# A two-part fp32 network on one core: the last attention's queries split tile by tile inside their projection, and another order of small steps at the layer ends

## The chip, the cores and the metric

The kernel runs on one core of a Trainium2 chip. A core has a matmul engine (TensorE, PE in the rows), a vector engine (VectorE, DVE), a scalar engine for activations (ScalarE, ACT), GpSimd (POOL), and SyncE (SP), which here issues the transfers. Each engine works through its own instructions in order; they meet at semaphores. The metric is the device time of one execution in microseconds. The matmul engine's clock is granted by a throttle and shown by the profile as a share of full speed: 1.00 is 2.4 GHz, 0.50 is 1.2 GHz.

## What is computed

Two blocks of a network in float32, with 512 tokens of width 1024 (and in the second block 256 context tokens). Shortened from the reference:

```python
def first_block(x, ...):
    h = x
    h = h + recurrent_block(h, ...)   # rmsnorm, w_in, gelu, causal conv, RG-LRU, w_out
    h = h + swiglu(h, ...)            # f0
    shared = shared_kv(h, ...)        # keys and values, plain and compressed
    h = h + nsa_layer(h, ..., *shared)  # w_in, q norm, rope, three attentions, w_out
    return h + swiglu(h, ...)         # f1

def rg_lru(x, gate_w, gate_b, lam):
    ...
    log_a = -LRU_C * jax.nn.softplus(-lam.astype(jnp.float32)) * r
    a = jnp.exp(log_a)
    ...

def modulate(x, shift, scale):
    return rms_norm(x) * (1 + scale) + shift

def odd_mixer(a_lat, a_ctx, rows, cols, w_in, sinks, w_out, ctx_out):
    ...
    q, k, v = split(a_lat @ w_in, s)  # 16 query heads, 2 key/value heads of 64
    q = axial_rope(q, rows, cols)
    k = axial_rope(k, rows, cols)
    ...
    o_lat, o_ctx = swa_heads(q, k, v, qc, kc, vc, sinks, ctx_out)
    return o_lat @ w_out, ...
```

The second block has an even layer (multi-head latent attention, MLA, and neighbourhood attention, NA, side by side, one output projection, swiglu g0), and an odd layer (sliding-window attention, SWA, over blocks of 128 queries, output projection, swiglu g1), then a last norm. Shifts, scales and gates of its layers come from `c` and `c_ctx` through the 6144-wide `mod_w`, the modulation.

## The kernel before

**Number form.** Every matmul takes its operands split into a high part, rounded to fp32r, and a low part, the rest. `mm3` makes three matmuls of one product (high by high, high by low, low by high), all recorded at L507.

**Weights.** They come as slabs of 128x1024 floats, 512 KB each. SyncE loads them in a fixed order into four places `RAW`; ScalarE's `high` (L430) writes the rounded half to `WH`, VectorE's `low` (L436) the rest to `WL`. `plan_of_weights` lists the slabs in their order. A call of `high` or `low` splits all slabs up to the one that `Slabs.upto` gives, three slabs ahead of the one it names. SyncE waits before each load until the last user of the place is done. Of the slabs, 96 are `mod_w`: they aren't split but read three times by VectorE in `mod_step` (L457, L460, L463), which does the modulation's product; `mod_passed` on ScalarE only goes past one in the order of splits. These steps stand inside the loops of f0, kv, the compression, b_out and f1.

**Order.** Each engine's program is written out by hand, stage by stage: functions `*_tensor`, `*_scalar`, `*_vector` are called in turn at the end. The stages are lru (`a_in`, gates, conv, scan, `a_out`), f0, kv, compression, q (`b_in`), nsa, b_out, f1, even (`e_in`, `e_v`, `q_up`), mla, na, e_out, g0, odd (`o_in`), swa, o_out, g1, out. `linear` makes one output tile of 128 features by up to 512 tokens, in one of three PSUM places; another engine must evacuate it before the place is used again.

**Lru.** VectorE evacuates `a_in` tiles 8 to 15 into the convolution (L972 to L978), then waits for ScalarE's Abs and Exp of lambda (L916, L918), runs a chain of small operations that makes `-8 softplus(-lam)` (L990 to L1015), and then evacuates the tiles of the gelu branch (L1029).

**Layer ends.** The last output projection of a stage runs by token parts. `turn_scalar` and `turn_vector` handle its end: `residual` (L700, L702) adds the PSUM tile to `H`; `square` (L638) and a matmul with ones give the sum of squares, `root` (L659, L662) the inverse root, and the loop over `kt` of 0 to 7 makes the normalised tiles (`normed_scaled` L682, `normed_high`, `normed_low`) that the next stage's first matmuls take. Between these steps the loop holds, for the next token part, the residuals of tiles 6 and 7 (at kt 2 and 5), the squares of tiles 5, 6, 7 (at kt 1, 3, 6), and the splits of the next slabs (at kt 1 and 4). In f1's last chunk `even_ahead_vector` and `even_ahead_scalar` prepare the context tokens of the even layer; the context itself is loaded once the last modulation step has left its vector's place.

**MLA and NA.** Both run rounds of scores, softmax, transposes and output. The first slabs of `e_out` are split by the call for `("mla_w", 0)` at s = 46 near the end of NA, between its softmax steps. `NB`, the neighbourhood biases, are loaded before the first of `e_out`'s late loads.

**Odd and SWA.** `o_in` gives tile 8 (keys), tiles 0 to 7 (two query heads each) and 9 (values). ScalarE copies a tile to a ring of three `TMP` places, VectorE makes its rotary form (L1093, L1095, L1097) in `QRAW2`. At the start of SWA `split_queries` makes 16 high halves on ScalarE (`query_high`, L1331) and 16 low halves on VectorE (`query_low`, L1336) into `Q2`. SWA then has 64 rounds, one for each block of queries and head: scores (L507), maximum (L2425), exponentials (L1393), transposes (L1402), evacuation (L1409), output, and flips of the outputs (L1436, L1442).

## Time and profile before

| | us |
|---|---|
| median of 3 runs | 3247.99 |
| the runs | 3247.99, 3265.96, 3245.41 |
| the profiled execution | 3253.99 |
| its span (first to last instruction) | 3251.9 |
| granted TensorE clock, mean over it | 0.965 |

The busy shares of the page say how much of the span each engine works; the shares of an engine that nothing waits for cost nothing. The chain is the work that ended last, followed back. In a timeline row the first number is the start in us from the span's start, the second the duration, and in brackets stands the engine's idle time just before, with what ended it. A trace is one execution; its terms are compared with its own time of 3253.99.

### The profile page before, as it was taken

Reading aid. Unit: us, or ns where it says so; the run is one execution under the profiler, and the core shown is the slowest. Engines: PE = TensorE matmul, PEld = TensorE weight load, DVE = VectorE, ACT = ScalarE, POOL = GpSimd, SP = SyncE. Lnnn points to the kernel's source line nnn. Section 1 sums busy time; section 2 is a strip of 40 time slices with the busy share of each in tenths; the row PEclk is TensorE's granted clock in tenths of the full one; section 3 lists DMA queues with packets and bytes.
Section 4 is the critical chain, followed back from the end, with each engine's and each line's share of the span. In section 5 each row is a group of like instructions: output and inputs, shape, how many; then the busy total and the mean of one; then the engine's idle time right before and its main releaser. Section 6 shows DMA issues by size and latency. Waiting matters only on the chain.

```text
span 3251.9 us, 41133 instructions
## 1 busy us (share of the span) xinstructions
PE 3032.2 (93%) x16349; PEld 2583.4 (79%) x16349; DVE 1656.7 (51%) x2849; ACT 1178.6 (36%) x2057; POOL 281.4 (9%) x274
## 2 busy tenths in 40 slices
PE   7899999888888999999898989999999989999999
PEld 5688888766778878878678878888888879888887
DVE  6756666656776666641345745222222645443333
ACT  3532223434663322241345643112112445432222
POOL 2310001001562000010000101000000100010001
PEclk9999999988999999999999989999999979999999
DMA  3235444240002445431000011111111200022231
GB/s 139 85 110 168 153 156 142 88 144 33 1 1 91 151 150 173 147 119 49 1 1 18 29 52 66 65 65 58 66 65 60 65 27 1 20 85 97 92 102 66
DMA packets 76287, 260.19 MB, mean 80 GB/s; under 512 B 8257, under 2 KB 12865, under 8 KB 75969
## 3 DMA queue, kind: packets, MB, share of 16 engines
q1 hardware_dynamic: 76096, 257.57, 23.9%
q8 instruction: 130, 2.13, 0.3%
q14 instruction: 61, 0.49, 0.0%
HBM read 255.44 MB, written 2.10 MB: 79 GB/s over the span
## 4 chain that ended last, share of the span: by engine, by line
PE 76%; DVE 8%; issue 6%; ACT 6%; POOL 2%; DMA 2%; DVEq 0%; SPq 0%; POOLq 0%; ACTq 0%
PE PS L507 73%; PE PS L1402 2%; POOL PB L1754 1%; ACT WH L430 1%; DVE WL L436 1%; DVE SM L2425 1%; DMA RAW<-in_f_in 1%; DVE TMP L682 1%; PE PS L1436 0%; ACT TMP L1409 0%; PE PS L1581 0%; ACT TMP L1393 0%; DVE RAW L463 0%; DMA RAW<-in_a_in 0%; ACT PB L1409 0%
## 5 line engine op out<-in xcount | busy, mean ns | idle before, releaser
L430 ACT ACTIVATE WH<-RAW 128x1024 fp32r<-128x1024 f32 (+1 forms) x367 | 379.4, 1036 | 859.5 <-PE PS L507 543.8
L507 PE MATMUL PS<-UH,WH 128*128 128x512 f32 (+1 forms) x1664 | 603.4, 363 | 52.3 <-DVE UL L962 12.4
L436 DVE TENSOR_TENSOR WL<-RAW,WH 128x1024 fp32r<-128x1024 f32 (+1 forms) x367 | 448.3, 1224 | 361.9 <-ACT WH L430 350.3
L507 PE MATMUL PS<-UL,WH 128*128 128x512 f32 (+1 forms) x1664 | 591.6, 356 | 0.0
L507 PE MATMUL PS<-UH,WL 128*128 128x512 f32 (+1 forms) x1664 | 588.6, 354 | 0.0
L507 PEld LDWEIGHTS PS<-UH,WH 128*128 128x128 f32 x1664 | 318.1, 191 | 108.8 <-DVE WL L436 31.1
L507 PEld LDWEIGHTS PS<-UL,WH 128*128 128x128 f32 x1664 | 318.1, 191 | 47.6 <-issue 5.8
L507 PEld LDWEIGHTS PS<-UH,WL 128*128 128x128 f32 x1664 | 317.0, 191 | 45.2
L648 POOL TENSOR_TENSOR ACC<-ACC,TMP 128x256 f32<-128x256 f32 (+1 forms) x108 | 115.0, 1080 | 2140.8 <-ACT TMP L638 2139.3
L507 PE MATMUL PS<-XSH,WH 128*128 128x512 f32 (+1 forms) x752 | 285.7, 380 | 15.3 <-DVE WL L436 5.8
L507 PE MATMUL PS<-XSL,WH 128*128 128x512 f32 (+1 forms) x752 | 284.2, 378 | 0.0
L507 PE MATMUL PS<-XSH,WL 128*128 128x512 f32 (+1 forms) x752 | 284.1, 378 | 0.0
L507 PE MATMUL PS<-HH,WH 128*128 128x512 f32 (+1 forms) x698 | 239.5, 343 | 2.6 <-DVE HL L2294 2.6
L507 PE MATMUL PS<-HL,WH 128*128 128x512 f32 (+1 forms) x698 | 239.1, 343 | 0.0
L507 PE MATMUL PS<-HH,WL 128*128 128x512 f32 (+1 forms) x698 | 237.5, 340 | 0.0
L835 DVE TENSOR_TENSOR TMP<-TMP,PS 128x512 f32<-128x512 f32 (+1 forms) x88 | 66.3, 753 | 301.1 <-PE PS L507 227.9
L702 DVE SCALAR_TENSOR_TENSOR H<-PS,MOD,H 128x512 f32<-128x512 f32 (+1 forms) x105 | 63.0, 621 | 242.5 <-PE PS L507 242.5
L507 PEld LDWEIGHTS PS<-XSH,WH 128*128 128x128 f32 x752 | 143.3, 191 | 43.5 <-DVE WL L436 10.6
L507 PEld LDWEIGHTS PS<-XSH,WL 128*128 128x128 f32 x752 | 143.2, 190 | 25.9
L507 PEld LDWEIGHTS PS<-XSL,WH 128*128 128x128 f32 x752 | 143.3, 191 | 25.5
L507 PEld LDWEIGHTS PS<-HH,WH 128*128 128x128 f32 x698 | 132.5, 190 | 19.4 <-DVE HL L2294 3.0
L507 PEld LDWEIGHTS PS<-HH,WL 128*128 128x128 f32 x698 | 132.1, 189 | 15.8
(349 smaller groups left out, 5396.9 us busy)
## 6 DMA issues: line engine op xcount, KB each, us to landing
RAW<-in_mod_w SPq DMA_DIRECT2D x96, 512.0 KB, 3.3
RAW<-in_f_in SPq DMA_DIRECT2D x88, 512.0 KB, 3.3
RAW<-in_g_in SPq DMA_DIRECT2D x88, 512.0 KB, 3.2
RAW<-in_f_out SPq DMA_DIRECT2D x32, 448.0 KB, 4.0
RAW<-in_g_out SPq DMA_DIRECT2D x32, 448.0 KB, 3.1
RAW<-in_a_in SPq DMA_DIRECT2D x16, 512.0 KB, 3.6
RAW<-in_f_out SPq DMA_DIRECT2D x16, 512.0 KB, 4.3
RAW<-in_g_out SPq DMA_DIRECT2D x16, 512.0 KB, 3.2
```

What stands on the lines that cost most here:

```text
L430: act.e.activation(hi, raw, ACT.Copy).then_inc(wh.step(n, i), 1)
L436: dve.e.tensor_tensor(lo, raw, hi.bitcast(F32), ALU.subtract).then_inc(wl.step(n, i), 1)
L507: return pe.e.matmul(out, l, r, start=start, stop=stop)
L648: pool.e.tensor_tensor(ACC[:, a:z], ACC[:, a:z], TMP[:, (kt - 1) % 3, a:z], ALU.add).then_inc(acc.step(key, p, kt), 1)
L682: dve.e.scalar_tensor_tensor(TMP[:, kt % 4, a:z], Hh[:, kt, a:z], gain(kt, a), RS[:, a:z], ALU.mult, ALU.mult).then_inc(xs.step(key, kt, p ...
L702: dve.e.scalar_tensor_tensor(Hh[:, m, a:z], o[:, c], g(m, a), Hh[:, m, a:z], ALU.mult, ALU.add).then_inc(res.step(stage, m, a), 1)
L835: dve.e.tensor_tensor(TMP[:, 2, 0:N], TMP[:, j % 2, 0:N], psum.at[tile][:, 0:N], ALU.mult).then_inc(dve_f.step(name, "mul", j), 1)
L1402: t = pe.e.transpose(o[:, 128 * j:128 * j + 128], b[:, col - lo:col - lo + 128], con("ident"))
L1754: pool.e.tensor_tensor(p, p, r.unsqueeze(2).to_broadcast([128, c, L]), ALU.mult).then_inc(scaled.step("nsa", n), 1)
L2425: dve.e.tensor_reduce(stat_of(n)[:, 0:1], psum.at["score", "swa", n][:, a:z], AX.X, ALU.max, negate=True).then_inc(most.step("swa", n), 1)
```

## The change

1. Lru: on both engines, one more slab, `a_in` 11, is split before the root. Abs and Exp of lambda go to the start of ScalarE's program, and VectorE's chain of small operations from behind the convolutions to before them.
2. Turns: the next part's residuals of tiles 6 and 7 at kt 0 and 2, its squares at kt 0, 2, 4, behind the splits of the next slabs, which go to kt 0 and 1.
3. Modulation: f1 holds 25 steps in its first loop where it held 32, none after j = 19; seven steps go to the q stage, one beside each of `b_in` 1 to 7.
4. Transfers: the last constants are loaded in front of `f1_in` 3 and no longer behind the context. Three `e_out` slabs are loaded in front of the biases.
5. Late in f1 VectorE prepares the context before the residuals, and ScalarE squares its last tile behind `normed_high`.
6. The look-ahead splits of `e_out` 0, 1, 2 go from s = 46 of NA to s = 9, 20, 31 of MLA.
7. Odd and SWA: the rotary form stays in the `TMP` ring, and each tile's two queries are split inside the `o_in` loop into `Q3`, a place of its own. `SKR` and `OST2` get other places; the flips and `OX` use `Q3`. Copies and evacuations wait accordingly.

Shortened to its core (VectorE's side is like ScalarE's, with `low` for `high`; the moved chain of lambda is not shown again):

```diff
+def mods_of(name, j):
+    if name == "f1":
+        return 0 if j > 19 else 2 if j % 3 == 0 and j > 3 else 1
+    return 2 if j % 3 == 0 or j in (10, 16) else 1
...
-    split("b_in", *range(9))
+    for i in range(9):
+        split("b_in", i)
+        if 0 < i < 8:
+            mod()
...
-    SKR = at("SKR", V0 + 15 * KB, [128, 768])
-    QRAW2 = at("QRAW2", V0 + 24 * KB, [128, 8, 512])
-    OST2 = at("OST2", V0 + 40 * KB, [128, 1024])
+    SKR = at("SKR", T0 + 12 * KB, [128, 768])
+    Q3 = at("Q3", V0 + 16 * KB, [128, 4, 16, 128], F32R)
+    OST2 = at("OST2", U0 + 44 * KB, [128, 1024])
...
+            if j == after("f1_in", 22):
+                sp.wait_ge(fin.after("nsa", 3, 3, 1))
+                sp.e.dma_start(CON[:, NC2:CONST_N], consts[:, NC2:CONST_N]).then_inc(s_con3, 16)
             if j == after("mod_w", 95):
                 sp.wait_ge(mod.after(95, 2))
                 sp.e.dma_start(CB, ctxT).then_inc(s_ctx, 16)
-                sp.wait_ge(fin.after("nsa", 3, 3, 1))
-                sp.e.dma_start(CON[:, NC2:CONST_N], consts[:, NC2:CONST_N]).then_inc(s_con3, 16)
...
     def turn_scalar(act, key, stage, Xd, shift, free, slabs_next):
...
-                if p + 1 < n and kt in (1, 3, 6):
-                    square(act, key, {1: 5, 3: 6, 6: 7}[kt], p + 1, h_ready, [])
                 if (p - n, kt) in slabs_next:
                     high(act, *slabs_next[p - n, kt])
+                if p + 1 < n and kt in (0, 2, 4):
+                    square(act, key, 5 + kt // 2, p + 1, h_ready, [])
...
     def turn_vector(dve, key, stage, tiles, g, h_before, Xd, gain, shift, free, slabs_next):
...
-                if p + 1 < n and kt in (2, 5):
-                    residual(dve, stage, tiles[1 + (kt == 5)], 6 + (kt == 5), p + 1, g, h_before)
                 if (p - n, kt) in slabs_next:
                     low(dve, *slabs_next[p - n, kt])
+                if p + 1 < n and kt in (0, 2):
+                    residual(dve, stage, tiles[1 + kt // 2], 6 + kt // 2, p + 1, g, h_before)
...
-        return {(-2, 1): (out[0], out[1] + 6), (-2, 4): (out[0], out[1] + 7), **({(-1, 1): first} if first else {})}
+        return {(-2, 0): (out[0], out[1] + 6), (-2, 1): (out[0], out[1] + 7), **({(-1, 1): first} if first else {})}
...
     def lru_scalar(act):
...
         logexp(act)
+        s1 = SM[:, 8:16]
+        act.e.activation(s1, vec("lam", 0, 8), ACT.Abs).then_inc(act_a.step("abs"), 1)
+        act.wait_ge(act_a.after("abs"))
+        act.e.activation(s1, s1, ACT.Exp, scale=-1.0).then_inc(act_a.step("lam"), 1)
...
+        high(act, "gate_w", 0, 1)
         root(act, "a", 0)
...
     def q_vector(dve):
...
+            if 0 < s < 8:
+                mod_step(dve, [dve_q.after("q", s - 3, "rope")] if s > 2 else [])
...
     def mla_scalar(act):
...
+            if s in AHEAD_AT:
+                high(act, "mla_w", 0, AHEAD_AT[s])
+    AHEAD_AT = {9: 2, 20: 1, 31: 0}
...
     def na_scalar(act):
...
-            if s == 46:
-                high(act, "mla_w", 0)
...
     def odd_scalar(act):
...
             if s > 2:
-                act.wait_ge(dve_q.after("o", s - 3, "rope"))
+                act.wait_ge(dve_q.after("o", 0, "rope"), *([dve_q.after("swa", s - 4, 1, "lo")] if s > 3 else []))
...
+            if s > 2:
+                odd_queries_scalar(act, s - 3)
         high(act, "o_in", 9)
+        odd_queries_scalar(act, 6)
+        odd_queries_scalar(act, 7)
...
     def odd_vector(dve):
...
-                roped(dve, "o", i, TMP[:, i % 3, :], 512, con("coss"), con("sins"), QRAW2[:, i - 1, :] if i else SKR[:, 0:512], [])
+                roped(dve, "o", i, TMP[:, i % 3, :], 512, con("coss"), con("sins"), TMP[:, i % 3, 0:512] if i else SKR[:, 0:512], [])
...
+            if 2 < s < 9:
+                odd_queries_vector(dve, s - 3)
         low(dve, "o_in", 9)
+        odd_queries_vector(dve, 6)
+        odd_queries_vector(dve, 7)
...
+    def odd_queries_scalar(act, i):
+        for j, (x, q3) in enumerate(odd_query(i)):
+            query_high(act, "swa", i, j, x, q3, [dve_q.after("o", i + 1, "rope")])
...
     def swa_scalar(act):
...
-        split_queries("swa", QRAW2, lambda i: [dve_q.after("o", i + 1, "rope"), lin.after("o_in", 9)], "act", act)
```

## Rows read from the trace of the kernel before

**Rows 1.** The page: busy us by engine, then engines' shares of the chain that ended last.

```profile
PE 3032.2 (93%) x16349; PEld 2583.4 (79%) x16349; DVE 1656.7 (51%) x2849; ACT 1178.6 (36%) x2057; POOL 281.4 (9%) x274
...
PE 76%; DVE 8%; issue 6%; ACT 6%; POOL 2%; DMA 2%; DVEq 0%; SPq 0%; POOLq 0%; ACTq 0%
```

**Rows 2.** Timeline of TensorE, recurrent layer: start, us, engine, line, operation, idle before and releaser.

```profile
40.55 0.77 PE L507 MATMUL PS<-UH,WH 128*128 128x512 f32 x1 [8.03 <-DVE TMP L972]
...
100.50 0.77 PE L507 MATMUL PS<-UH,WH 128*128 128x512 f32 x1 [9.49 <-DVE Y L1029]
```

**Rows 3.** Timeline of TensorE: the first and the last of four turns.

```profile
193.28 0.36 PE L507 MATMUL PS<-UH,WH 128*128 128x256 f32 x1 [3.21 <-DVE H L700]
...
2876.97 0.55 PE L507 MATMUL PS<-XSH,WH 128*128 128x256 f32 x1 [3.70 <-DVE H L702]
```

**Rows 4.** Timeline of TensorE, f1: first and last of three waits, then the turn.

```profile
1077.20 0.50 PE L507 MATMUL PS<-XSH,WH 128*128 128x512 f32 x1 [1.48 <-DVE WL L436]
...
1317.85 0.50 PE L507 MATMUL PS<-XSH,WH 128*128 128x512 f32 x1 [1.33 <-DVE WL L436]
...
1401.57 0.80 PE L507 MATMUL PS<-ACC,CON 128*128 128x256 f32 x1 [5.07 <-POOL ACC L648]
```

**Rows 5.** Timelines of TensorE and ScalarE at the end of NA.

```profile
1900.94 1.12 PE L1436 MATMUL PS<-CON,NBC 128*128 128x128 f32 x4 [8.87 <-ACT RS L1409]
...
1894.70 1.06 ACT L430 ACTIVATE WH<-RAW 128x1024 fp32r<-128x1024 f32 x1 [4.83 <-DMA RAW<-in_e_out]
...
1899.62 0.90 ACT L1393 ACTIVATE TMP<-PS,SM 128x768 f32<-128x768 f32 x1 [2.63 <-DVE SM L2247]
```

**Rows 6.** Timelines of TensorE, ScalarE and VectorE: SWA's start, and one projection tile.

```profile
2652.06 0.58 PE L507 MATMUL PS<-SKH,Q 128*128 128x256 f32 x1 [9.06 <-ACT PB L1393]
...
2638.48 10.42 ACT L1331 ACTIVATE Q<-QRAW 64x512 fp32r<-64x512 f32 x16
...
2639.14 11.45 DVE L1336 TENSOR_TENSOR Q<-QRAW,Q 64x512 fp32r<-64x512 f32 x16 [14.35 <-ACT Q L1331]
...
2600.41 0.69 DVE L1093 TENSOR_TENSOR TMP<-PS,CON 128x512 f32<-128x512 f32 x1 [3.10 <-PE PS L507]
```

**Rows 7.** Windows: stretch, us, busy of PE, PEld, DVE, ACT, POOL, clock, DMA, GB/s.

```profile
193.68:197.09 3.41, 3.41 (x18) 3.41 (x17) 0.61 (x2) 0.30 (x1) 0.00 (x0) 0.50 0.33 127
1900.94:1921.29 20.35, 14.63 (x65) 12.72 (x65) 3.17 (x12) 7.55 (x13) 0.00 (x0) 0.50 0.17 61
2652.06:2671.76 19.70, 19.70 (x95) 19.70 (x96) 6.34 (x17) 8.55 (x25) 0.00 (x0) 0.50 0.00 1
2667.51:2671.05 3.54, 3.54 (x19) 3.54 (x18) 1.05 (x3) 1.44 (x4) 0.00 (x0) 0.50 0.00 0
2686.66:2688.82 2.16, 2.10 (x19) 1.96 (x18) 0.94 (x4) 1.33 (x4) 0.00 (x0) 1.00 0.00 0
```

**Rows 8.** Timelines of VectorE and ScalarE, recurrent layer.

```profile
38.57 1.23 DVE L436 TENSOR_TENSOR WL<-RAW,WH 128x1024 fp32r<-128x1024 f32 x1 [3.29 <-issue]
...
91.85 1.28 ACT L918 ACT_TABLE_LOAD   x1
...
93.38 0.17 DVE L990 TENSOR_SCALAR SM<-SM 128x8 f32<-128x8 f32 x1 [5.50 <-ACT SM L918]
```

**Rows 9.** Timeline of VectorE: the residual ahead of the first turn's wait.

```profile
192.71 0.42 DVE L700 TENSOR_TENSOR H<-PS,H 128x256 f32<-128x256 f32 x1
```

**Rows 10.** The chain that ended last, around the even turn.

```profile
1383.19 6.60 DMA H<-in_ctxT
```

**Rows 11.** Timeline of SyncE's queue as f1 starts.

```profile
1050.03 13.02 SPq L471 DMA_DIRECT2D RAW<-in_f_in  x2
```

**Rows 12.** Timeline of VectorE in the q stage.

```profile
743.34 0.75 DVE L1086 SCALAR_TENSOR_TENSOR TMP<-PS,SM,TMP 128x512 f32<-128x512 f32 x1 [3.33 <-ACT TMP L1081]
```

**Rows 13.** Groups of VectorE by line, 1000 to 1400 us: count, busy, mean ns, idle before.

```profile
L463 DVE CUSTOM_DVE_ANT_1 RAW<-RAW,H,VECS 128x1024 f32<-128x1024 f32 x43 | 55.3, 1285 | 1.5
...
L460 DVE CUSTOM_DVE_ANT_1 TMP<-RAW,H,MOD 128x512 f32<-128x512 f32 x43 | 33.4, 776 | 1.5
```

More of the change, by code:

```diff
@@ L176, in ffn @@
                 if step:
-                    mod()
-                    if j % 3 == 0 or j in (10, 16):
+                    for _ in range(mods_of(name, j)):
                         mod()
@@ L412, in body, with splits_until @@
     split_at = {"act": 0, "dve": 0}
-    def splits_until(which, name, idx):
-        a, z = split_at[which], slabs.upto[slabs.index[name, idx]]
+    def splits_until(which, name, idx, short=0):
+        a, z = split_at[which], slabs.upto[slabs.index[name, idx]] - short
         split_at[which] = max(a, z)
@@ L424, in split_places, with high @@
         return name, idx, hi[:, 0:n], lo[:, 0:n], raw_of(name, idx)[:, 0:n], [] if old is None else [lin.after(*slabs.plan[old][0:2])]
-    def high(act, name, idx):
-        for j in splits_until("act", name, idx):
+    def high(act, name, idx, short=0):
+        for j in splits_until("act", name, idx, short):
             n, i, hi, _, raw, used = split_places(j)
@@ L430, in high, with low @@
             act.e.activation(hi, raw, ACT.Copy).then_inc(wh.step(n, i), 1)
-    def low(dve, name, idx):
-        for j in splits_until("dve", name, idx):
+    def low(dve, name, idx, short=0):
+        for j in splits_until("dve", name, idx, short):
             n, i, hi, lo, raw, used = split_places(j)
@@ L453, in mod_step @@
         low(dve, "mod_w", j)
-        dve.wait_ge(loaded("mod_w", j), act_a.after("cond"), dve_a.after("mod_b", 3))
+        dve.wait_ge(loaded("mod_w", j), act_a.after("cond"), dve_a.after("mod_b", 3), *free)
         if j:
@@ L479, in sync_engine @@
         after = lambda *slab: slabs.issued[slabs.index[slab]]
-        first_late = next(j for j, old in enumerate(slabs.old) if old is not None and slabs.plan[old][0] == "e_out")
+        first_late = next(j for j, old in enumerate(slabs.old) if old is not None and slabs.plan[old][0] == "e_out" and slabs.plan[old][1] > 2)
         for j in range(3, len(slabs.plan)):
@@ L848, in ffn_vector @@
                 low(dve, *tile)
+                if c == 2 and name == "f1":
+                    even_ahead_vector(dve, m)
                 if m < 5 or not ends:
@@ L914, in lru_scalar @@
         gates_scalar(act, 7)
-        s1 = SM[:, 8:16]
-        act.e.activation(s1, vec("lam", 0, 8), ACT.Abs).then_inc(act_a.step("abs"), 1)
-        act.wait_ge(act_a.after("abs"))
-        act.e.activation(s1, s1, ACT.Exp, scale=-1.0).then_inc(act_a.step("lam"), 1)
         act.e.activation(IDR[:, :], con("ident"), ACT.Copy).then_inc(act_a.step("idr"), 1)
@@ L1015, in lru_vector @@
         dve.e.tensor_scalar(NSP, s4, -8.0, None, ALU.mult).then_inc(done, 1)
+        low(dve, "gate_w", 0, 1)
+        low(dve, "gate_w", 1)
+        for m in range(8):
+            b, o = TMP[:, m % 4, :], XR[:, m, :]
+            dve.wait_ge(rstd.after("a", 0))
+            if m > 3:
+                dve.wait_ge(dve_a.after("conv", m - 4, 3))
+            dve.e.memset(b[:, 0:3], 0.0).then_inc(dve_a.step("pad", m), 1)
+            dve.wait_ge(lin.after("a_in", 8 + m))
+            dve.e.tensor_tensor(b[:, 3:515], psum.at["a_in", 8 + m][:, 0:512], RS[:, 0:512], ALU.mult).then_inc(dve_a.step("x", m), 1)
+            psum.leave(("a_in", 8 + m), dve_a)
+            dve.wait_ge(dve_a.after("pad", m), dve_a.after("x", m))
+            dve.e.tensor_scalar(o, b[:, 0:512], vec("conv_w", m), vec("conv_b", m), ALU.mult, ALU.add).then_inc(dve_a.step("conv", m, 0), 1)
+            for k in (1, 2, 3):
+                dve.wait_ge(dve_a.after("conv", m, k - 1))
+                dve.e.scalar_tensor_tensor(o, b[:, k:k + 512], vec("conv_w", 8 * k + m), o, ALU.mult, ALU.add).then_inc(dve_a.step("conv", m, k), 1)
+            low(dve, "a_in", 8 + m)
         def decay(m):
@@ L1452, in flipped_hi @@
     def flipped_hi(q):
[L1453 removed]
+        return lambda m: Q3[:, q, m:m + 4, :]
     def flipped_lo(q):
[L1456 to L1467 removed]
+        return lambda m: Q3[:, q, 8 + m:12 + m, :]
     Wave = namedtuple("Wave", "g q rows L tiles first last")
@@ L2132, in mla_vector @@
                     rotary_low(dve, h + 1)
+            if s in AHEAD_AT:
+                low(dve, "mla_w", 0, AHEAD_AT[s])
     def na_gpsimd(pool):
@@ L2480, in scalar_engine @@
         out_scalar(act, "o_out", "g1", False, of_mods(1, 3), ("g1_in", 0))
-        ffn_scalar(act, "g1", 512, [], "out", False)
+        ffn_scalar(act, "g1", 512, [lin.after("o_out", 7)], "out", False)
         turn_scalar(act, "out", ("g1", 2), None, None, [], next_slabs(("g1_out", 16), None))
```

60 lines of the change are left out of this document (17 added, 43 removed).

## The prediction

> **What bounds the kernel.** I read the page's busy shares and its chain first. The reader is to see that TensorE (PE) is busy 93% of the span of 3251.9 us and carries 76% of the chain; no other engine comes near [rows 1]. So only two things can move the end: time in which TensorE waits, and time in which it runs at the lower of its two clock levels, 1.2 instead of 2.4 GHz. Next I listed, on TensorE's timeline, every wait over 0.35 us with its releaser, and looked in the window view at the granted clock behind each. The large waits are few and each lies in a place that the change touches: two in the recurrent layer's start [rows 2], one at the head of each of four layer turns [rows 3], four in the second feed-forward layer f1 and the turn behind it [rows 4], one at the end of the neighbourhood attention (NA) [rows 5], one at the start of the last attention (SWA) [rows 6]. Behind each, the clock stands at 0.50 for some us: the windows of 3.41 us behind a turn and of 20.35 and 19.70 us behind the two attention waits show it [rows 7].
>
> **The change part by part**, in us gained.
>
> 1. *Split of a_in slab 11 before the root.* TensorE waits 8.03 until 40.55. It starts 0.75 after VectorE's split that ended at 39.80, and that split stood idle for 3.29, since its slab could be loaded only when a_in 11, its place's last user, was split behind the root [rows 2, 8]. With a_in 11 split earlier the load is no longer last; ScalarE's two remaining splits (1.06 each, [rows 5]) and VectorE's 1.23 follow the root, which ends at about 31.3 (8.5 before the VectorE split's end). That gives 31.3 + 2.1 + 1.2 + 0.75 = 35.4, and with 0.7 for the start of the chain 36.1. Gain **4.4** (3.3 to 5.2).
>
> 2. *Lambda's chain to the front.* VectorE idles 5.50 for ScalarE's Abs and Exp, then runs 26 small operations from 93.38 to 98.6, and TensorE waits 9.49 for the evacuation queued behind them [rows 2, 8]. Moved, they lie under the first loads, where both engines have nothing to do. The wait of 9.49 and the 2.2 lost behind it at the half clock go, but the decay and scan work behind it stays as long as it was and TensorE comes to it sooner: its next wait grows by about 3.7 in my reading. Gain **8.0** (4 to 11.7). The moved Abs and Exp need no further table load at the front if they stand in the set that the logarithm has loaded; a load is 1.28 and the Exp starts at its end [rows 8]. By the Trainium skill, "ScalarE: Activation LUTs", "What ACT_TABLE_LOAD costs", a switch is 1.28 us plus a drain of 1.38; the row shows the 1.28 and no drain after it, and by the page the 5.50 would hold 2.66 for the switch instead of 1.28. In both readings it is part of the 5.50 that goes, so it changes the reading of that wait and not the sum.
>
> 3. *Turns: the next part's residuals at steps 0 and 2 instead of 2 and 5, squares likewise.* Four turns wait 3.21, 3.60, 3.22 and 3.70 for the residual of the last tile, 13.7 together [rows 3]. In the first, that residual (0.42 long) starts at 192.71, and the matmul at 193.28 [rows 9]; three steps of the normalising loop earlier is 3 us earlier. I leave 0.7 of each wait: 13.7 - 2.8 = 10.9. Each is followed by 3.41 us at 0.50 [rows 7], which at the full clock take half: 4 x 1.65 = 6.6. The smaller turn behind the odd layer's attention gives 1.5 by its own two waits of 1.6. Sum **19.0**. Below: 0, if the order only passes the wait on (a rival). The splits of the next slabs move from steps 1 and 4 to 0 and 1: 1.2 each on VectorE, ahead of the residual, covered by matmuls that already have their slabs; without that cover it is one split, 1.2, per turn.
>
> 4. *f1 with 25 modulation steps in its loop instead of 32.* Three waits on the low half of a slab's split, from 1.48 to 1.33 with 2.96 between, 5.8 together [rows 4], come where two modulation steps stand between two splits on VectorE. With one step in nearly all iterations they go; the half clock behind the longest gives 1.5. Gain **7.3** (3 to 7.3).
>
> 5. *The even turn.* TensorE waits 5.07 for the sum of squares of the context [rows 4], whose load, 6.60 long, is on the page's chain there [rows 10]. The load waits for the last modulation step, which comes two iterations sooner. The constants' load that stood behind it in the queue goes to 1050 us; there the queue's two issues of 13.02 us are waiting for places, and the transfer engines have nothing [rows 11], so it costs nothing; without that cover it is the 6.60 of the load of the same size. Gain 5.07 and 1.9 of clock, **7.0** (3 to 7).
>
> 6. *e_out's first three splits out of the end of NA.* The wait of 8.87 ends with the last head's exponentials, and ahead of these ScalarE waits 4.83 for e_out's load and then splits, VectorE likewise [rows 5]. Taken away, softmax work is next in line at once. The whole 8.87 goes; of 14.63 us of TensorE work at 0.50 behind it [rows 7], which would take 7.3 at the full clock, I take a little over half of the 7.3, 4.0, since the low clock lasted after each turn too [rows 7]. Gain **12.9** (8.9 to 16.2). The same splits in MLA are three times 1.06 on ScalarE and 1.23 on VectorE, each about half busy there: **-1.5** (0 to -3).
>
> 7. *SWA's query splits into the projection.* Before, 16 splits on ScalarE (10.42) and 16 on VectorE (11.45) stand between the projection and the scores, and TensorE does its first transposes at 2652.06, after a wait of 9.06 for the first exponentials [rows 6]. In the projection VectorE idles 3.10 in each tile [rows 6], so two splits of 0.72 hide; ScalarE, with two of 0.65, has still less to do. Behind the projection two tiles' splits are left beside ScalarE's evacuation and its table load. In before, the first split on ScalarE started behind both of these, at 2638.48 [rows 6]; there the first exponentials can start now, and with 2.0 for them and for what leads to the transposes (estimated from 0.90 for one set of them in the NA rows [rows 5]) these come at 2640.5. Gain 11.5. Behind it TensorE runs 19.70 us at 0.50, in which a round is 3.54 long instead of 2.16 [rows 7]: 5.6 rounds, 7.7 at most. I take **3.0** of it, for the same reason as at NA. Together **14.5** (11.5 to 19.2). The copy of tile s now waits for the split of tile s - 4; behind it on ScalarE stands the evacuation that frees a place for TensorE, but that split is over a tile old by then.
>
> 8. *Seven modulation steps into the q stage* (b_in 1 to 7). A step's three passes are 1.29, 0.78 and, of the same form, 0.78 again, with their starts 2.87 [rows 13]; VectorE idles 3.33 per tile there [rows 12]. It fits with 0.4 to spare: 0 (-5 to +1). *Tail*: the last residuals take their new order there too, where nothing covers them; one residual of 0.42 [rows 9] is the bound, I take **-0.3**.
>
> Sum: 4.4 + 8.0 + 19.0 + 7.3 + 7.0 + 12.9 + 14.5 - 1.5 - 0.3 = 71.3. The profiled run took 3253.99 and would take 3182.7; it is 6.0 above the median of 3247.99, which gives **3176.7 us**.
>
> **Rivals.**
>
> *A: the clock does not follow.* At NA's end and SWA's start the waits go but TensorE goes on at 1.2 GHz: 4.0 + 3.0 back, 3183.7. For it: in [rows 7] TensorE worked 19.70 us without a gap at 0.50 before it rose. Against: it did rise. By the Trainium skill, "TensorE: Matmul & The Clock Gate", "A second HAM failure mode: psum-queue depth-cycling", short idles between groups of matmuls make the clock go back and forth; by that rule the sum would be this rival's 3183.7. No row of before shows such a return in the attention's rounds.
>
> *B: the turns pay elsewhere.* The earlier residuals keep VectorE from a normalised tile that is next in TensorE's order, so each turn's wait returns further on: 19.0 back, 3195.7. For it: VectorE runs both in order. Against: the residual costs 0.42 and the matmuls already handed over last longer.
>
> *C: the q stage overflows.* A modulation step does not fit into 3.33 with its two extra waits, or the slab loads it needs come late: seven times 1 to 2 us, 3190.
>
> *D: SWA's splits still end last*, because the last two queries' splits and the table load follow the projection: 14.5 back, 3191.
>
> *E: slower.* Tile by tile splits thin TensorE's work at SWA's start so that its clock stays at 0.50 through the stage. A round is then 3.54 instead of 2.16 [rows 7]; 64 rounds cost up to 88 us, 3176.7 + 88 = 3265. It outweighs the gain once more than 71.3 / 1.38 = 52 of the 64 rounds run low. Against: the clock rose at 2671.76 after a worse start.
>
> **How the numbers follow.** Forecast 0.55, A 0.20, B 0.12, C 0.05, D 0.05, E 0.03. The low end is the forecast with the upper bounds of parts 2, 6 and 7 (3.7, 3.3 and 4.7), 3165, and 5 more for clock that I gave no term: 3160. The high end takes in A to D and two of them together: 3205. A measurement of this kernel tells about 1%, 32 us, from no change. Faster by more than that needs 32 of the 71.3: all but E and three bad terms at once, 0.90; within 1%, 0.07; slower, 0.03.
>
> **What would show it.** In the profile after: no TensorE wait over 1 us for a residual (L700, L702) at the turns; first wait of 8.03 down to 3 to 4; none of 9.49; the VectorE splits of f1 never last; first flip of NA directly behind its last scores; SWA's first transposes 2 to 3 us behind the projection's end; the granted clock up from 0.965 towards 0.98. Wrong would be: waits of 2 us or more in b_in tiles on mod junk or slabs, a wait on the context's load still over 3, or the clock at 0.50 for 10 us or more at either attention.

## The result: 1.5% faster, and where the time went

The changed kernel's median is 3202.02 us (3195.20 to 3213.82, 4 runs) against 3250.11 for the kernel before. The ratio is 0.9847, with a 95% interval of 0.9802 to 0.9893. Executed again beside other kernels it was 3198.69 us (3188.85 to 3204.78), ratio 0.9845 (0.9821 to 0.9869). The forecast was 3176.7, with a range of 3160 to 3205. So the direction was right and the time lies in the range, 3 to 6 us below its upper end, but 46 to 50 us came where 71 were forecast. The profiled execution took 3198.71 us, with a span of 3196.6.

The page of the changed kernel, the lines that answer to [rows 1]:

```profile
PE 3018.4 (94%) x16349; PEld 2571.3 (80%) x16349; DVE 1659.3 (52%) x2849; ACT 1178.3 (37%) x2056; POOL 286.5 (9%) x274
...
PE 49%; DVE 3%; ACT 3%; issue 2%; DVEq 0%; ACTq 0%
```

The chain here could be followed back over 57% of the span only, so its 49% don't compare with the 76% of before.

TensorE issues the same 16349 matmuls in both kernels, in the same order. That gives the best view of all for such a change: take from both timelines the start of matmul number n, and compare stretch by stretch. The table is worked out from the starts in the two timelines, in us. The sum over all stretches is the difference of the spans, 55.3; those left out come to -0.4.

| matmuls | what lies there | before | after | gain | forecast |
|---|---|---|---|---|---|
| start to 200 | first loads, first projection of lru | 77.4 | 77.0 | 0.3 | 4.4 |
| 200 to 380 | gates' end, gelu tiles | 54.3 | 42.5 | 11.8 | 11.7 |
| 380 to 640 | decay, scan, a_out | 51.7 | 58.5 | -6.8 | -3.7 |
| 640 to 760, 2380 to 2500, 4500 to 4620, 12500 to 12700, 14580 to 14800 | five turns | 127.0 | 113.0 | 14.0 | 19.0 |
| 2900 to 3340 | q stage into nsa | 131.9 | 127.5 | 4.4 | 0 |
| 4620 to 6080 | f1 | 332.4 | 324.5 | 7.9 | 7.3 |
| 6080 to 6240 | even turn | 42.0 | 35.2 | 6.8 | 7.0 |
| 7000 to 8100 | MLA | 178.5 | 187.6 | -9.1 | -1.5 |
| 8100 to 9060 | NA | 167.6 | 149.5 | 18.2 | 12.9 |
| 9060 to 12500 | e_out, g0 | 601.8 | 603.3 | -1.5 | 0 |
| 13060 to 13300 | SWA's start | 51.4 | 33.9 | 17.5 | 14.5 |
| 13300 to 14340 | the rest of SWA | 137.1 | 144.7 | -7.7 | 0 |

Two lines stand out: MLA and the rest of SWA give back 17 us, of which the forecast had 1.5.

TensorE's timeline after shows what became of the waits of [rows 2], [rows 3] and [rows 6]: start, us, engine, line, operation, then idle before and its releaser. The line numbers are the changed kernel's.

```profile
37.27 0.47 PE L517 MATMUL PS<-UH,WH 128*128 128x512 f32 x1 [3.50 <-DVE TMP L1019]
...
49.38 1.22 PE L517 MATMUL PS<-XR,RAW 128*128 128x512 f32 x1 [3.33 <-DVE TMP L1019]
...
135.70 0.79 PE L517 MATMUL PS<-YH,WH 128*128 128x512 f32 x1 [6.90 <-DVE YL L1051]
...
185.85 0.36 PE L517 MATMUL PS<-UH,WH 128*128 128x256 f32 x1 [1.15 <-DVE H L710]
...
2592.79 0.35 PE L517 MATMUL PS<-SKH,Q 128*128 128x256 f32 x1 [0.99 <-ACT VS L2350]
...
2595.80 0.58 PE L517 MATMUL PS<-SKH,Q 128*128 128x256 f32 x1 [1.66 <-ACT PB L1407]
```

The wait of 8.03 is 3.50, that of 9.49 is gone, and 6.90 stands at the next one (2.77 in before). A turn's 3.21 is 1.15. At SWA's start 4.28 and 9.06 have become 0.99 and 1.66. In NA the flips now follow the last scores directly, with waits of 0.78 where 8.87 stood [rows 5].

The new wait in MLA, with what stands before it on ScalarE and VectorE:

```profile
1640.32 0.80 PE L517 MATMUL PS<-CKH,QLH 128*128 128x512 f32 x1 [3.80 <-ACT TMP L1407]
...
1634.26 0.83 ACT L1898 ACTIVATE QRS<-QR 32x768 fp32r<-32x768 f32 x1
1635.12 0.84 ACT L1899 ACTIVATE QRS<-QR 32x768 fp32r<-32x768 f32 x1
1635.98 1.06 ACT L439 ACTIVATE WH<-RAW 128x1024 fp32r<-128x1024 f32 x1
1639.27 0.90 ACT L1407 ACTIVATE TMP<-PS,SM 128x768 f32<-128x768 f32 x1 [2.23 <-DVE SM L2120]
...
1637.14 1.23 DVE L445 TENSOR_TENSOR WL<-RAW,WH 128x1024 fp32r<-128x1024 f32 x1 [3.81 <-ACT WH L439]
1638.28 0.95 DVE L2120 TENSOR_REDUCE SM<-PS 128x1 f32<-128x768 f32 x1
```

Read it backwards. TensorE waits for exponentials, these for a maximum (L2120) on VectorE, and this one stands in order behind the split of an e_out slab, which waits for ScalarE's half. ScalarE makes that half only after two rotary halves of 0.83 us. VectorE has been idle for 3.81 us, and the last matmul of the maximum's scores ended at about 1635.5. A split costs 1.23 us of VectorE; in this round it costs TensorE 3 us.

### The profile page after: what moved, and what is told of

It is laid out like the page before. It is cut to its first block, busy times and chain, and to the rows that moved or that the text cites. A ratio compares the mean times of both kernels' runs of the same rounds, so it can differ in the third digit from the quotient of the medians.

```text
span 3196.6 us, 41132 instructions
## 1 busy us (share of the span) xinstructions
PE 3018.4 (94%) x16349; PEld 2571.3 (80%) x16349; DVE 1659.3 (52%) x2849; ACT 1178.3 (37%) x2056; POOL 286.5 (9%) x274
## 3 DMA queue, kind: packets, MB, share of 16 engines
q8 instruction: 130, 2.13, 0.3%
## 4 chain that ended last, share of the span: by engine, by line
PE 49%; DVE 3%; ACT 3%; issue 2%; DVEq 0%; ACTq 0%
PE PS L517 47%; PE PS L1416 2%; DVE SM L2450 0%; PE PS L1450 0%; ACT TMP L1423 0%; DVE PS L2250 0%; DVE SM L2120 0%; ACT TMP L1407 0%; ACT WH L439 0%; DVE QRS L1905 0%; DVE NKL L2174 0%; ACT PB L1423 0%; ACT PB L1407 0%; ACT N L2159 0%; DVE WL L445 0%
## 5 line engine op out<-in xcount | busy, mean ns | idle before, releaser
L445 DVE TENSOR_TENSOR WL<-RAW,WH 128x1024 fp32r<-128x1024 f32 (+1 forms) x367 | 446.4, 1220 | 340.2 <-ACT WH L439 329.3
L517 PEld LDWEIGHTS PS<-UH,WL 128*128 128x128 f32 x1664 | 316.4, 190 | 45.2
L517 PEld LDWEIGHTS PS<-HH,WH 128*128 128x128 f32 x698 | 132.6, 190 | 19.2 <-DVE HL L2299 2.8
```

Source lines behind the costliest of these rows:

```text
L445: dve.e.tensor_tensor(lo, raw, hi.bitcast(F32), ALU.subtract).then_inc(wl.step(n, i), 1)
L517: return pe.e.matmul(out, l, r, start=start, stop=stop)
```

## The experiments

### The same kernel again, and a trade undone

**The changed kernel once more.**

> The changed kernel once more, unaltered. In its first profile the stage by stage sum gives 55.5 us over before, but holds two long stretches at the lower TensorE clock behind small waits: 10.3 us in MLA (1680.8 to 1691.1) and 20.5 us in SWA (2728.7 to 2749.2), where before's profile has none and 3.4. Theory 1 (these stretches come and go from execution to execution): they are absent or elsewhere here, and the span lies within 3188 to 3212 without a code cause. Theory 2 (they belong to the new order, since the change puts splits in MLA and another place for the queries in SWA): both stand at the same instructions again, 10 and 20 us long.

Measured: 3198.69 us, span of the profile 3186.7. SWA in the window view, its three stretches (matmuls 13060, 13300, 14000, 14340), first in the changed kernel's first profile, then in this one. Columns: stretch, us, busy of PE, PEld, DVE, ACT, POOL, granted clock, DMA share, GB/s.

```profile
2586.95:2620.87 33.92, 30.69 (x242) 29.06 (x242) 11.23 (x32) 17.87 (x50) 0.00 (x0) 0.95 0.01 1
2620.87:2712.85 91.98, 87.58 (x702) 86.12 (x701) 46.75 (x136) 52.12 (x140) 0.00 (x0) 0.94 0.00 1
2712.85:2765.59 52.74, 48.75 (x342) 47.78 (x342) 20.55 (x63) 26.62 (x74) 0.00 (x0) 0.81 0.00 1
```

```profile
2581.34:2621.01 39.67, 36.89 (x242) 36.31 (x242) 11.65 (x32) 18.41 (x50) 0.00 (x0) 0.74 0.00 1
2621.01:2712.31 91.30, 86.29 (x702) 84.89 (x701) 46.64 (x135) 51.51 (x140) 0.00 (x0) 0.96 0.00 1
2712.31:2758.18 45.87, 41.71 (x343) 39.89 (x342) 20.15 (x63) 25.95 (x76) 0.00 (x0) 0.96 0.00 1
```

The waits at SWA's start are equal in both (0.99 and 1.66), yet in one profile the clock is low behind them for 3.4 us and in the other for 20.5. In the last quarter it is the other way round. One and the same code has both, so theory 1 holds for SWA. In MLA it fails: the wait of 3.80 and a low stretch of 10.2 us some 40 us later stand at the same matmuls in both, and 7000 to 8100 takes 187.6 and 188.3. That loss belongs to the code.

**The look-ahead splits back in NA.**

```diff
-            if s in AHEAD_AT:
-                high(act, "mla_w", 0, AHEAD_AT[s])
...
+            if s == 46:
+                high(act, "mla_w", 0)
```

With them the biases are again loaded before the first late `e_out` slab (part 4).

> The changed kernel with the look-ahead splits of e_out 0, 1, 2 back at s = 46 of NA, biases loaded first as in before. Theory 1 (the part is a trade, and its cost in MLA was mis-sized): NA's end loses the 15 us that it gained (its wait of about 8.9 is back), MLA wins back 4 to 5 us, 3.1 of it at the wait of 3.80 before the scores of round 22 and 1.3 at the wait of 2.06; the whole is 10 us slower than the changed kernel. Theory 2 (MLA's loss of 9 us in the first profile is clock alone): the wait of 3.80 stays, MLA's length stays within 2 us of the changed kernel's, and the whole is 15 us slower.

Measured: 3196.66 us (3192.52 to 3197.65), ratio 0.9839 (0.9823 to 0.9856). By stretches NA's end (8880 to 9060) loses 16.8 us and MLA wins 10.4, of which 3.3 is the wait (3.80 against 0.51), 1.2 a second wait at the stage's end (2.06 against 0.89) and the rest low clock at 1640 and 1681. The trade is worth 6.4 us, not 11.4 as forecast. The earlier part of NA (8100 to 8880) takes 3 us more here as well, but over the 13 profiles it varies between 114.4 and 119.9 without regard to where these splits stand, so it is left out. By the whole time nothing of the trade is seen. In the profiled execution this is because SWA took 169.2 us where the changed kernel needed 178.6 and 176.8; for the other executions it is not known. Part 6 of the change, placed as it is, gains nothing that can be told by the whole time. Neither theory had MLA's size right: 10 us hang on it, not 4 to 5.

**The splits in rounds with room.**

```diff
-    AHEAD_AT = {9: 2, 20: 1, 31: 0}
+    AHEAD_AT = {9: 2, 17: 1, 29: 0}
```

> The changed kernel with the three look-ahead splits at s = 9, 17 and 29 of MLA instead of 9, 20 and 31: rounds in which neither ScalarE nor VectorE has a rotary or latent split. Theory 1 (at s = 20 VectorE's split waits in order for ScalarE's, which stands behind two rotary halves of 0.83 us each, and the next round's maximum stands behind both): the wait of 3.80 at about 1640 falls to 0.7 to 1.0, the clock stretch behind it goes, gain 3 to 5 us over the changed kernel. Theory 2 (any round is hurt by a split, each engine being busy half the time): a wait of 2 to 4 us appears in round 18 or 19 instead, no gain.

Measured: 3193.61 us (3183.92 to 3199.53), ratio 0.9830 (0.9806 to 0.9853). MLA takes 180.7 us instead of 187.6. TensorE's wait for the same scores, and the window in which the changed kernel had 0.88 of the clock (second fence):

```profile
1636.09 0.50 PE L517 MATMUL PS<-CKH,QLH 128*128 128x512 f32 x1 [0.51 <-ACT TMP L1407]
...
1640.00:1690.00 50.00, 44.56 (x317) 38.97 (x317) 23.50 (x56) 24.30 (x51) 0.00 (x0) 1.00 0.04 11
```

```profile
1640.00:1690.00 50.00, 45.19 (x281) 39.38 (x281) 22.12 (x53) 23.53 (x50) 0.00 (x0) 0.88 0.09 31
```

3.80 has become 0.51, and with the wait both low stretches went, the one right behind it and the one 40 us later. That is theory 1, and 6.9 us in this stage instead of the 3 to 5 expected. 8.9 were won, 3.3 of them the wait's own and the rest mostly clock, and 2.0 were lost, 1.0 in each of the two rounds that took the splits, where new waits of 1.33 and 1.34 stand (around matmuls 7400 and 7650). No wait of 2 us has appeared there. All seven profiles with a split at s = 20 have 187.1 to 188.7 for this stage, and `flips_apart`, the other one with 9, 17, 29, has 180.8. By the whole time the 5 to 8 us between the medians are not clear of the spread.

### SWA

**The queries split behind the projection again.** The edit takes back `Q3`, the in-loop splits and their waits (part 7 alone).

> The changed kernel with the queries of the last attention kept after rotation and split in one go behind the projection, as in before (places and waits of before too). Theory 1 (the 17.8 us gained at SWA's start in the first profile pair are this part's, and what follows it in SWA is clock by chance): the wait of 9 us and the low clock at the start are back, 15 to 18 us slower than the changed kernel at SWA's start, and the low stretch of 20.5 us in SWA's third quarter is not tied to it. Theory 2 (the query place Q3 is what brings the 6.9 us lost in SWA's second half): the start loses 17 and the second half wins 7, 8 to 11 us slower.

Measured: 3202.92 us (3200.41 to 3203.51), ratio 0.9862 (0.9843 to 0.9880). TensorE's wait is back:

```profile
2605.41 0.58 PE L517 MATMUL PS<-SKH,Q 128*128 128x256 f32 x1 [9.07 <-ACT PB L1407]
```

The start takes 48.6 us instead of 33.9 (or 39.7), the rest of SWA 134.4 instead of 144.7 (or 137.2). By the medians taking part 7 back costs 1 to 4 us, within what these runs can tell, and less than either theory said (15 or 8 us and more).

**The query splits alone, on the kernel before.**

> The kernel before with the query splits inside the projection alone. Theory 1 (10.7 us of waiting go at SWA's start, and the lower clock behind takes back up to 7 by chance): matmuls 13060 to 13300 take 33.9 or 40 to 41 us instead of 51.4, SWA's later stretches stay at 88 to 92 and 46 to 54, and the whole is 6 to 17 us faster than before. Theory 2 (the new place and its waits cost in the rounds behind): 13300 to 14340 takes over 142 in this profile (137.1 in before) and the whole gains under 5.

Measured: 3239.80 us (10 runs), ratio 0.9967 (0.9947 to 0.9987), which is 11 us (4 to 17). The start took 33.9 us, the rest 144.9. So 17.5 us went at one place and 7.9 came back in the same stage, as in the changed kernel's first profile. Whether that return belongs to the new place of the queries, as theory 2 has it, can be read from all the profiles. The table gives the length of SWA's three stretches; the waits at its start are 13.3 us together in the upper three and 2.65 or less in the lower.

| kernel | start | middle | last | SWA |
|---|---|---|---|---|
| before | 51.4 | 91.2 | 45.8 | 188.4 |
| swa_back | 48.6 | 88.0 | 46.3 | 183.0 |
| flips_alone (below) | 52.8 | 87.3 | 45.2 | 185.3 |
| swa_alone | 33.9 | 91.1 | 53.8 | 178.8 |
| changed kernel | 33.9 | 92.0 | 52.7 | 178.6 |
| again | 39.7 | 91.3 | 45.9 | 176.8 |
| ahead_in_na | 33.9 | 88.2 | 47.1 | 169.2 |
| ahead_free_rounds | 41.0 | 88.2 | 54.3 | 183.4 |
| turn_order_back | 33.9 | 92.0 | 51.4 | 177.3 |
| lru_back | 41.0 | 91.6 | 57.1 | 189.7 |
| mods_back | 33.9 | 92.0 | 47.0 | 172.9 |
| a11_late | 39.7 | 91.3 | 45.9 | 176.8 |
| flips_apart | 33.9 | 87.3 | 45.3 | 166.5 |

Nine profiles have the queries split early and the flips as in the change: 169.2 to 189.7, mean 178.2. The two with late splits have 188.4 and 183.0, mean 185.7. The gain of part 7 is therefore about 7.5 us with a spread of 20 between executions, against 14.5 forecast. With the flips apart (below) the one pair of profiles gives more, 185.3 with late and 166.5 with early splits. Theory 2 of swa_alone, by its stretch, came true (144.9 is over 142), but the whole gained more than its 5 us, and its reason fails: in `again` and `a11_late` the same SWA code does it in 137.2.

**The flips apart.** The low stretches in SWA's middle and last part begin behind the flips of a finished block of queries, but for two of 13.7 us (in `lru_back` and `mods_back`). There TensorE makes four transposes, waits 1.50 us until VectorE has emptied the place, and makes four more. The edit puts a round of matmuls between the two groups, on all three engines, and keeps the splits at 9, 17, 29:

```diff
-            n = s - 4
-            if 0 <= n < len(SWA) and SWA[n][1] == 15:
-                flip_tensor(pe, ("swa", SWA[n][0]), OST2, 8, [fin.after("swa", n)])
+            for n, first, nm in ((s - 5, 4, 8), (s - 4, 0, 4)):
+                if 0 <= n < len(SWA) and SWA[n][1] == 15:
+                    flip_tensor(pe, ("swa", SWA[n][0]), OST2, nm, [fin.after("swa", n)], first)
```

> The changed kernel with e_out's look-ahead splits at s = 9, 17, 29 and, new, the two groups of four flip transposes behind each block of queries in SWA one round apart, so that TensorE does a round's matmuls between them. Theory 1 (the flips' wait of 1.50, with 0.96 behind it, starts the lower clock in SWA's third quarter, 3.4 to 24 us long in the profiles so far): the waits at the first three flips fall under 0.5, the low stretches behind them go, the stretch of matmuls 14000 to 14340 takes 43 to 45 us each time instead of 45.8 to 54.3, and the whole is 4 to 10 us faster than with the splits alone (3193.6). Theory 2 (the lower clock there comes by itself): the waits go and 3 to 4 us with them, but 14000 to 14340 still takes over 50 in some profiles.

Measured: 3173.24 us (3170.56 to 3185.12, 5 runs), ratio to before 0.9769 (0.9745 to 0.9792). It is the fastest version, 25 to 29 us faster than the changed kernel and 20 faster than `ahead_free_rounds`, where theory 1 had 4 to 10. SWA's stretches:

```profile
2573.10:2607.03 33.93, 31.74 (x243) 30.24 (x242) 11.23 (x32) 17.86 (x50) 0.00 (x0) 0.90 0.00 1
2607.03:2694.33 87.30, 83.28 (x702) 81.80 (x701) 46.45 (x135) 50.73 (x140) 0.00 (x0) 1.00 0.01 1
2694.33:2739.58 45.25, 40.74 (x342) 38.81 (x342) 20.04 (x63) 26.04 (x76) 0.00 (x0) 1.00 0.01 1
```

The last two have the full clock throughout. The waits at the flips are now two of 0.73 to 0.97 each, where one of 1.50 and one of up to 0.96 stood (one of them below). They did not fall under 0.5 as theory 1 said; what went is mostly the clock's part. Behind the last block, where no round is left to put between, the two groups still stand together, with a wait of 1.51, and there 6.8 us at the lower clock follow.

```profile
2666.60 0.74 PE L1416 MATMUL PS<-CON,PB 128*128 128x128 f32 x5 [0.73 <-DVE Q L1462]
```

Not all of the 20 us is shown to be the flips'. The spans of the two profiles differ by 20.7, of which 9.9 lie in SWA's middle and last part and 7.1 in its start, which the edit doesn't touch. Against the mean of the nine profiles with the flips together, the middle and last part are 8.8 us shorter (132.6 against 141.4).

**The flips apart, alone on the kernel before.**

> The kernel before with one edit: SWA's two groups of four flip transposes one round apart. Theory 1 (the flips' waits start the lower clock in SWA, whatever the rest of the kernel is): the three stretches of matmuls 13060 to 13300, 13300 to 14000 and 14000 to 14340, 51.4, 91.2 and 45.8 us in before, become 51 (unchanged, its wait of 9 us stays), 87 to 88 and 45, and the whole is 4 to 6 us faster than before; the 20 us of the version with the flips apart over the one without are then mostly the long stretches that the changed kernel had in SWA's last quarter. Theory 2 (the gain needs the other parts): no change within 2 us.

Measured: 3244.10 us (10 runs), ratio 0.9988 (0.9968 to 1.0008): 4 us, not clear of zero. The middle fell from 91.2 to 87.3, the last stretch from 45.8 to 45.2, and both are free of low stretches, as in `flips_apart`. The expected sizes of theory 1 came, 4.5 us for these two. The long stretches that cost 7 to 12 us in the last part of some profiles did not occur in before's, so there was little more to win there. The two versions with the flips apart have no low stretch in the middle and last part, and all 11 other profiles have at least one of 3.4 us or more. That is shown for one profile of each version (two of the changed kernel), not for many executions.

### The other parts, undone one at a time

**The turn order.**

> The changed kernel with the old order inside the turns alone: residuals at steps 2 and 5, squares at 1, 3, 6, slab splits at 1 and 4. Theory 1 (the turns' gain is this order's): in TensorE's order the stretches around the turns lose 3.5, 2.1, 3.6, 3.5 and, in the odd layer's turn, 2.9 us, 15 to 16 together, and the waits of 3.2 to 3.7 on a residual stand there again. Theory 2 (part of it is from the other parts, since the even turn's 6.8 hangs on squares too): two or more of these stretches stay within 1 us of the changed kernel's, or the even turn loses more than 1.

Measured: 3212.46 us (2 runs), ratio 0.9880 (0.9852 to 0.9908). The five turns lose 3.6, 3.1 (4.6 against `again`), 3.6, 2.9 and 1.9 (3.5): 15 to 18 us. The even turn stays at 35.24. Theory 1.

**The recurrent layer as before.**

> The changed kernel with the recurrent layer as in before: a_in 11 split behind the root, Abs, Exp and the chain for lambda behind the convolutions. Theory 1 (the chain only hands on its time to the decay and scan work): the stretch of matmuls 200 to 380 loses 11.8 us and 380 to 640 wins 6.8 back, 5.0 slower; the first 200 matmuls lose 0.7 to 4, since the wait of 8.03 comes back but the one of 3.33 at about 49 goes. Theory 2 (the 6.8 lost behind it is the lower clock of 10.2 us there, chance): 380 to 640 wins back at most 3, and the whole is 9 or more slower.

Measured: 3213.72 us (2 runs), ratio 0.9884 (0.9854 to 0.9914). 200 to 380 takes 54.7 instead of 42.5. 380 to 640 takes 54.5 with a low stretch of 6.8 us; before and the two `alone` kernels have 51.7 without one, and the nine profiles with the new order 57.2 to 58.7, each with a low stretch of 6.8 to 10.2 us. So 12.0 go and 5.6 come back (58.0 against the mean of 52.4), 6.3 net. The 5.6 are 4.1 of wait (6.90 against 2.77) and the clock behind it. The 4.0 that 380 to 640 wins back here lie between the two theories. The whole is 12 to 15 us slower than the changed kernel, as theory 2 said, but in the profile 11 to 13 us of the difference stand in SWA (189.7), whose code is the same.

**a_in 11 split late, the rest of the change kept.**

```diff
-        high(act, "gate_w", 0, 1)
...
-        low(dve, "gate_w", 0, 1)
```

> The changed kernel without the early split of a_in slab 11, the lambda chain staying at the front. Theory 1 (the early split is worth what the forecast gave it, 4.4 us, and the first profile showed less because its first loads landed later and its lower-clock stretch fell at another wait): TensorE's second wait is 8.0 again and the first 200 matmuls take 65 us, against 60.7 to 64.3 with the split. Theory 2 (the wait only moves to the convolution at about 49 us): the first 200 matmuls take 62 to 64 and the wait at about 50 us is under 1.

Measured: 3193.38 us (2 runs), ratio 0.9836 (0.9799 to 0.9872), not to be told from the changed kernel. The first wait is 8.0 again and the second 2.0:

```profile
40.16 0.76 PE L517 MATMUL PS<-UH,WH 128*128 128x512 f32 x1 [7.98 <-DVE TMP L1017]
...
51.37 0.70 PE L517 MATMUL PS<-XR,RAW 128*128 128x512 f32 x1 [2.00 <-DVE TMP L1017]
```

Counted from the first matmul, the first 200 take 66.1 us. The five profiles without the early split have 65.0 to 66.1, mean 65.5; the eight with it 60.7 to 64.4, mean 62.5. The split is worth 3 us on average and 0.7 between before's profile and the changed kernel's first, where the convolution's wait was 3.33 and a low stretch stood behind it; in `again` they were 2.17 and none there. Both theories hold in part.

**The modulation steps and the constants back.**

> The changed kernel with the modulation steps where before had them (none in the q stage, 32 in f1's first loop) and the constants loaded behind the context again. Theory 1 (seven steps hide in the q stage and their absence frees f1 and the even turn): f1 loses 7.9 us, the even turn 6.8, the stretch of b_in stays within 0.5. Theory 2 (the q stage pays for them): the stretch of matmuls 2900 to 3340, where the changed kernel is already 3 to 4 shorter than before, becomes shorter by another 1 to 3.

Measured: 3203.41 us (2 runs), ratio 0.9852 (0.9824 to 0.9880), 1 to 5 us slower than the changed kernel. f1 takes 329.2 instead of 324.5, the even turn 43.1 instead of 35.2. f1's loss is 4.7, not 7.9: its longest wait, 2.96 in before, is 1.24 here. The two kernels `flips_alone` and `swa_alone`, whose f1 is before's unchanged, take 329.3 and 329.2 as well, so 3 us of before's profile belonged to that execution. And the q stage with its seven steps is faster, not slower: 2900 to 3340 takes 130.4 here, 127.3 to 128.6 in the nine profiles with them, and 130.0 to 131.9 in before and the two `alone` kernels. A slab of `mod_w` takes a place in the look-ahead and needs no split, so fewer splits stand ahead of the first q tile: in before VectorE does three in a row there, after two with room between.

## Why the forecast was right, and where its terms were not

The sum of the parts as the experiments size them is 3.1 + 6.3 (lru) + 16.6 (turns, the middle of 15.1 to 18.2) + 4.7 (f1) + 7.9 (even) + 6.4 (e_out's splits) + 7.5 (SWA) + 2.3 (q stage, 130.4 against the mean of 127.5 and 128.6) - 0.2 (tail) = 54.6. It agrees with the measured 35 to 64 and 43 to 58 us of the two intervals. That is a weak check. The terms are read from one or a few profiles each, and the whole times of the kernels with a part undone give less: by their ratios against 0.9846 the turns are worth 11 us, lru 12, the modulation steps with the constants 2, SWA 5 and e_out's splits -2, together 28 of the 50, each known to no better than about 10 us.

That the time fell into the range is in part luck. The range reached up to 3205 to take in the rivals A to D and two of them together; none of B, C and D came, and most of what did come were costs in MLA and in SWA's clock for which the forecast had less room. Of the signs named, a wait on a residual at the turns over 1 us still stands at four of them, and one sign of being wrong came, the clock at 0.50 for 10 us or more at an attention (20.5 us in SWA). Against the forecast's steps:

1. *What bounds the kernel* (TensorE's waits and its clock): right. Nearly every wait named is gone or smaller, by about the size said.
2. *Part 1*: right mechanism. 4.4 was forecast, 3.1 is the mean. The step left out the next wait at the convolution, 2.0 in before, up to 3.33 after.
3. *Part 2*: 9.49 + 2.2 was 12.0, right. The part handed back was sized 3.7 and is 5.6, for want of clock: the step counted the next wait's growth (4.1) but no low stretch behind it.
4. *Part 3*: 19.0 against 16.6. The waits left are 1.15, 1.86, 1.15 and 1.49 and not 0.7. Rival B (turns gain nothing) is out.
5. *Part 4*: 7.3 against 4.7. The step took a wait of 2.96 and the low clock behind it from one profile; in three other profiles of that code the stretch is 3 us shorter.
6. *Part 5*: 7.0 against 7.9. Constants and context loads were hidden as said.
7. *Part 6*: this is the first failed term. NA's end gained 16.8 where 12.9 was said; its low clock of 30.7 us fell to 3.4 to 6.8, so rival A is wrong there. But the three splits in MLA, put at 1.5 with a bound of 3 because both engines are half idle, cost 10.4. The working took busy shares where the order mattered: at s = 20 the split stands behind two rotary halves on ScalarE and ahead of the next maximum on VectorE. It needed the question which the other parts asked, what is queued behind the waiting instruction and who waits for that. Of the 10.4, 1.2 are a wait that goes with GpSimd's work on the biases (last section), and the run that undid them moved splits and load order together, so it doesn't tell which of the two they belong to.
8. *Part 7*: the second failed term. The waits fell by 10.7, near the 11.5. (The matmul at 2652.06 that the forecast calls the first transposes is by its row, `PS<-SKH,Q`, one of the scores, which waits for the exponentials too; the size is not changed by it.) The clock's 3.0 was not there on average; instead the low clock that before had at the start returned, for 3.4 to 23.9 us at the start and up to 27.3 in the last quarter, so 7.5 of 14.5 stayed. That is rival A's mechanism, in one of its two places, at more than its price of 3.0. Rival E (the whole stage low) did not come, nor D.
9. *Part 8*: 0 was forecast with -5 to +1, and 2.3 were gained, above that bound; rival C is out.

The two failed terms are 5.0 (part 6: 11.4 against 6.4) and 7.0 (part 7), 12.0 of the 16.7 us between 71.3 and 54.6. The last 4 to 8 between this sum and the measured gain lie within the intervals.

By the Trainium skill, "TensorE: Matmul & The Clock Gate", "A second HAM failure mode: psum-queue depth-cycling", frequent short idles between groups of matmuls make the clock go back and forth; this stood beside rival A. The profiles agree in SWA's middle and last part: low stretches of 3.4 to 27.3 us come behind flip waits of 1.50 and go with them, but for the two of 13.7 us. In NA's end no run shows it. On the Trainium skill's figure for a table load's drain ("ScalarE: Activation LUTs", "What ACT_TABLE_LOAD costs") nothing in the sum depended: the wait of 9.49 went whole.

What stays open: why about the same waits at SWA's start are followed by 3.4 to 6.8 us at the lower clock in six profiles and by 20.5 to 23.9 in four. The runs show only that both occur in the same code. Open too is how much of the last version's 20 us is the flips'.

## What to carry to other kernels

Where two kernels issue the same matmuls in the same order, compare the starts of matmul n, stretch by stretch; it showed gains and what was given back that no whole time could. A step moved into an engine that is half idle is not free: look in its new round for what stands ahead of it on the first engine and behind it on the second, and pick a round without its like (here 6.9 us of the stage for two changed numbers). And on a kernel that TensorE bounds, hunt waits of 1 to 2 us in the middle of dense work as well: a round of matmuls put between two groups of transposes, at three places, took about 9 us from SWA in the changed kernel and 4.5 in the kernel before. The waits themselves became only 0.5 to 0.8 us shorter at each place.

## What the runs showed of the hardware that was not expected

The granted clock falls behind waits as short as 1.50 us. In `mods_back` a stretch of 13.7 us at 1.2 GHz even begins behind waits of 0.65 and 0.69 us, with none over 0.7 in the 25 us before:

```profile
2767.42 0.63 PE L1404 MATMUL PS<-CON,PB 128*128 128x128 f32 x4 [0.65 <-ACT TMP L1411]
...
2769.58 1.09 PE L1404 MATMUL PS<-CON,PB 128*128 128x128 f32 x4 [0.69 <-ACT PB L1411]
```

And in the same code the stretch at 1.2 GHz that follows is sometimes 3.4 us long and sometimes over 20. The four runs of the changed kernel spread over 18.6 us with mean clocks of 0.968 to 0.975.

VectorE's instructions are longer where GpSimd works beside it. In the changed kernel a split that takes 1.23 us takes 2.31, and a pair of small low halves that takes 1.93 takes 4.98 (VectorE's rows, then GpSimd's of the same time):

```profile
109.18 2.31 DVE L445 TENSOR_TENSOR WL<-RAW,WH 128x1024 fp32r<-128x1024 f32 x1
...
1639.85 1.93 DVE L1905 TENSOR_TENSOR QRS<-QR,QRS 32x768 fp32r<-32x768 f32 x2
...
1714.07 4.98 DVE L1905 TENSOR_TENSOR QRS<-QR,QRS 32x768 fp32r<-32x768 f32 x2
...
109.06 16.72 POOL L1070 TENSOR_TENSOR SG<-SG,XR 128x512 f32<-128x512 f32 x8 [0.95 <-ACT SG L941]
...
1713.38 4.86 POOL L2149 TENSOR_TENSOR NB<-NB,CON 128x896 f32<-128x896 f32 x2 [329.65 <-DMA NB<-in_relb]
```

The second case stands ahead of TensorE's last wait in MLA, 2.06 us. Where GpSimd begins earlier, its work overlaps the pair less: in before the pair took 3.73 and the wait was 0.80, and in `ahead_in_na` they were 3.83 and 0.89 (VectorE's row, then GpSimd's):

```profile
1703.73 3.83 DVE L1905 TENSOR_TENSOR QRS<-QR,QRS 32x768 fp32r<-32x768 f32 x2
...
1701.60 4.16 POOL L2145 TENSOR_TENSOR NB<-NB,CON 128x896 f32<-128x896 f32 x2 [319.01 <-DMA NB<-in_relb]
```

GpSimd's row is released by the load of the biases. In the four profiles whose kernels load them ahead of the late `e_out` slabs (and split the first three in NA), GpSimd begins 2.0 to 2.1 us ahead of the pair, which takes 3.73 to 3.83, with waits of 0.79 to 0.89. In the nine others it begins 0.6 to 0.9 us ahead, with 4.76 to 5.07 and 1.83 to 2.13. No run took GpSimd's work away, so this is read from the times standing side by side and not tested by itself.
